# Feed-forward entries in halves, one split on GpSimd, and a narrower z panel in a two-layer hybrid block

## What is computed

```python
def first_block(x, positions, ...):
    h = x
    for l in range(DEPTH):                       # DEPTH = 2
        h = layer_norm(DEEPNORM_ALPHA * h + 0.5 * swiglu(h, ffn1_w_gate[l], ffn1_w_up[l], ffn1_w_down[l]), ...)
        mix = hybrid_mixer(h, cos, sin, w_in[l], ...)
        h = layer_norm(DEEPNORM_ALPHA * h + mix, ln2_g[l], ln2_b[l])
        h = layer_norm(DEEPNORM_ALPHA * h + 0.5 * swiglu(h, ffn2_w_gate[l], ffn2_w_up[l], ffn2_w_down[l]), ...)
    return h

def swiglu(x, w_gate, w_up, w_down):
    return (jax.nn.silu(x @ w_gate) * (x @ w_up)) @ w_down

def hybrid_mixer(x, ...):
    proj = x @ w_in                              # 1024 x 6856, cut by column
    (dq, dk, dv, dz, da, dbeta, glu, c_q, c_kv, k_r, gate_logits) = jnp.split(proj, ...)
    ...

def ada_params(c, w, b):                         # the second model's modulation
    mod = jax.nn.silu(c) @ w + b                 # c: one row of 1024; w: 1024 x 3072
```

## Time and profile before

| | |
|---|---|
| median of 3 runs | 3070.93 us (3068.96 to 3071.79) |
| the profiled execution: its own time, and its span | 3071.66 us, 3069.9 us |
| busy PE, PEld | 2913.4 us (95%), 2467.8 us (80%) |
| busy DVE, ACT, POOL | 2016.9 us (66%), 1454.4 us (47%), 50.7 us (2%) |
| mean granted TensorE clock | 0.976 |
| queue of instruction fetches | 75 packets, 1.23 MB |

### The profile page before, as it was taken

One profiled execution on the slowest core, in us unless ns is written; L12 is line 12 of the kernel. 1 busy time (PEld: TensorE's weight loads), 2 busy tenths in 40 slices (PEclk: granted clock), 3 DMA queues, 4 the chain that ended last, 5 costly groups with the idle time before them and its releaser, 6 DMA issues.

```text
span 3069.9 us, 44687 instructions
## 1 busy us (share of the span) xinstructions
PE 2913.4 (95%) x16782; PEld 2467.8 (80%) x16782; DVE 2016.9 (66%) x2457; ACT 1454.4 (47%) x1612; POOL 50.7 (2%) x93
## 2 busy tenths in 40 slices
PE   7999988899899998899999999988999999999997
PEld 7998886599899988758988699455878887888786
DVE  6767863477767788327761454144898789878987
ACT  5444521254444452214430344133776767666765
POOL 2000010000000001000000000000000000000000
PEclk9999999999899999999999999998999999999999
DMA  8754512486677433136743455313999999999995
GB/s 292 237 174 162 154 67 84 134 274 222 221 247 246 152 121 110 57 110 225 254 150 137 137 192 176 111 69 136 359 338 329 339 348 337 329 339 349 337 330 213
DMA packets 396808, 659.84 MB, mean 215 GB/s; under 512 B 12011, under 2 KB 239193, under 8 KB 396697
## 3 DMA queue, kind: packets, MB, share of 16 engines
q1 hardware_dynamic: 396696, 658.32, 62.3%
HBM read 657.23 MB, written 1.05 MB: 214 GB/s over the span
## 4 chain that ended last, share of the span: by engine, by line
PE 70%; DVE 10%; PEld 5%; issue 5%; ACT 4%; DVEq 2%; DMA 2%; PEldq 1%; ACTq 1%; SPq 0%
PE banks L711 18%; PE banks L712 17%; PE banks L713 17%; PE banks L2091 3%; PE banks L2123 3%; PE banks L1389 2%; PE banks L707 1%; PE banks L784 1%; DVE mod_sum L1045 1%; DVE expert_rest L1113 1%; PEld banks L1225 1%; DVE ffn_arena L1052 1%; PE banks L885 1%; DVE panel_rest L1740 1%; PE banks L879 1%
## 5 line engine op out<-in xcount | busy, mean ns | idle before, releaser
L711 PE MATMUL banks<-ffn_arena 128*128 128x256 f32 (+1 forms) x3460 | 1165.0, 337 | 42.8 <-DVE ffn_arena L1073 16.3
L713 PE MATMUL banks<-ffn_arena 128*128 128x256 f32 (+1 forms) x3460 | 1149.4, 332 | 0.0
L711 PEld LDWEIGHTS banks<-ffn_arena 128*128 128x128 f32 x3460 | 661.3, 191 | 117.0 <-issue 38.4
L713 PEld LDWEIGHTS banks<-ffn_arena 128*128 128x128 f32 x3460 | 660.9, 191 | 69.4
L1113 DVE TENSOR_TENSOR expert_rest<-expert_raw,ffn_arena 128x2048 fp32r<-128x2048 f32 (+1 forms) x306 | 646.4, 2161 | 85.9 <-ACT ffn_arena L972 81.5
L712 PE MATMUL banks<-ffn_arena 128*128 128x256 f32 (+1 forms) x2200 | 672.8, 306 | 0.0
L972 ACT ACTIVATE ffn_arena<-expert_raw 128x2048 fp32r<-128x2048 f32 (+1 forms) x306 | 538.9, 1815 | 110.4 <-PE banks L713 107.1
L712 PE MATMUL banks<-expert_rest,ffn_arena 128*128 128x512 f32 (+1 forms) x1224 | 465.9, 381 | 0.0
L712 PEld LDWEIGHTS banks<-ffn_arena 128*128 128x128 f32 x2200 | 423.9, 193 | 17.4 <-issue 0.5
L1052 DVE TENSOR_TENSOR ffn_arena<-gate_w,ffn_arena 128x1024 fp32r<-128x1024 f32 x110 | 130.0, 1223 | 212.0 <-ACT ffn_arena L908 212.0
L712 PEld LDWEIGHTS banks<-expert_rest,ffn_arena 128*128 128x128 f32 x1224 | 230.0, 188 | 42.8
(11 more groups left out here) (415 smaller groups left out, 3521.6 us busy)
## 6 DMA issues: line engine op xcount, KB each, us to landing
expert_raw<-in_moe_w_gate_dram SPq DMA_DIRECT2D x90, 1024.0 KB, 5.2
expert_raw<-in_moe_w_up_dram SPq DMA_DIRECT2D x90, 1024.0 KB, 5.4
expert_raw<-in_moe_w_down_dram SPq DMA_DIRECT2D x90, 1024.0 KB, 5.0
gate_w<-in_ffn_w_gate_dram SPq DMA_DIRECT2D x55, 1024.0 KB, 5.4
up_w<-in_ffn_w_up_dram SPq DMA_DIRECT2D x55, 1024.0 KB, 5.4
down_w<-in_ffn_w_down_dram SPq DMA_DIRECT2D x55, 1024.0 KB, 5.4
mod_unit<-in_mod_w_dram SPq DMA_DIRECT2D x48, 1024.0 KB, 5.1
panel<-in_w_in_dram SPq DMA_DIRECT2D x44, 1024.0 KB, 5.7
```

What stands on the lines that cost most here:

```text
L711: mm(out, w[0], x[0], start=start, stop=False)
L713: return mm(out, w[1], x[0], start=False, stop=stop)
```

## The change

Six things are done:

1. The loop over the two layers is written out (`for l in range(DEPTH)`) on every engine, so the waits compare against constants.
2. The second tile enters a feed-forward in halves of 512 columns: L1182 is two instructions, with a new count (`norm_half`) after the first; PE turns four blocks behind each, ACT copies each half, DVE subtracts each half.
3. The first gate panel of three of the four feed-forwards in the first model (not of the very first) is split earlier: ACT's pass stands between the layer norm's two square roots, and the low part is computed by GpSimd.
4. The modulation sums at the boundary of the two layers are no longer ahead of the turns: 12 of the 24 matmuls stand between the two tiles, 12 behind the second. ACT's copy of them, and a wait of DVE for them, now stand ahead of the first up panel.
5. The first step of each feed-forward is taken out of DVE's loop, with the modulation unit behind `unit_vec` and up low instead of ahead of them.
6. The eight logits move from the z panel (520 to 512 columns) to the last panel (192 to 200 columns, as a DMA of its own with runs of 32 bytes); their 16 matmuls are gone. One of two filler matmuls at the second entry is gone too.

```diff
-    + [("z", [("w_in", 0, D, C_Z, 520)]),
+    + [("z", [("w_in", 0, D, C_Z, PANEL)]),
        ("lora", [("w_in", 0, D, C_CQ, PANEL)]),
-       ("lora", [("w_in", 0, D, C_CQ + PANEL, C_GATE - C_CQ - PANEL)])]
+       ("rope_decay", [("w_in", 0, D, C_KR - PANEL // 4, KR_COLS), ("w_in", 0, D, C_Z + PANEL, 2 * HEADS)])]
...
-            with pool.Fori(0, DEPTH) as l:
+            for l in range(DEPTH):
...
+                for first in (l * FFN_LAYER + NS, l * FFN_LAYER + FFN_LAYER)[:2 if l + 1 < DEPTH else 1]:
+                    for i, half in enumerate((slice(0, KD // 2), slice(KD // 2, KD))):
+                        pool.wait_ge(gate_high, first * 2 + i + 1)
+                        last = nc.gpsimd.tensor_tensor(gate_parts[1][:, half, :], gate_w[:, half, :], gate_parts[0][:, half, :].bitcast(F32), ALU.subtract)
+                    last.then_inc(gate_low, 1)
...
-        def turn_h(pe, done, fill=0):
+        def turn_h(pe, done, fill=0, mod=None):
             for t in range(TT):
                 if t == 1 and fill:
                     spin(5, fill)
-                pe.wait_ge(norm_done, done + t + 1)
+                if t == 1 and mod is not None:
+                    mod_pe(pe, mod, banks[:, 0, 0:12], range(12))
+                if t == 0:
+                    pe.wait_ge(norm_done, done + 1)
                 for half in range(2):
+                    if t == 1 and half == 0:
+                        pe.wait_ge(norm_half, done // 2 + 1)
+                    elif t == 1:
+                        pe.wait_ge(norm_done, done + 2)
...
+            if mod is not None:
+                mod_pe(pe, mod, banks[:, 0, 12:24], range(12, 24)).then_inc(mod_col_done, 1)
...
         def turned_act(act, before):
-            for t in range(TT):
-                act.wait_ge(turned, before + 2 * t + 2)
-                act_fn(x_parts[0][:, :, t * P:(t + 1) * P], turned_tile(t), ACT.Copy).then_inc(x_high, 1)
+            act.wait_ge(turned, before + 2)
+            act_fn(x_parts[0][:, :, 0:P], turned_tile(0), ACT.Copy).then_inc(x_high, 1)
+            for half, done in ((slice(0, 4), x_half), (slice(4, 8), x_high)):
+                act.wait_ge(turned, before + 2 + half.stop // 4)
+                act_fn(x_parts[0][:, half, P:], turned_tile(1)[:, half, :], ACT.Copy).then_inc(done, 1)
...
-            with dve.Fori(0, NS - 1) as s:
+            gate_vec(dve, n, 1)
+            unit_vec(dve, n, 0, FB * SEQ)
+            up_vec(dve, n, 1)
+            if m is not None:
+                mod_vec(dve, m, 1, slice(MOD_COLS, 2 * MOD_COLS))
+            down_vec(dve, n, 0)
+            dve.wait_ge(unit_high, n + 1)
+            tt(unit_parts[1], act_t, unit_parts[0].bitcast(F32), ALU.subtract).then_inc(act_ready, 1)
+            with dve.Fori(1, NS - 1) as s:
                 step(s)
...
-            tile = v3(panel_ready(5), 0, KD, 520)
-            for t in range(TT):
-                for k in range(KD):
-                    mm(small_bank[:, 8 * t:8 * t + 8], HT[:, k, t * P:(t + 1) * P], tile[:, k, 512:520],
-                       start=k == 0, stop=k == KD - 1)
             pe.drain().then_inc(panel_used, 1)
...
-            with pe.Fori(0, DEPTH) as l:
+            for l in range(DEPTH):
                 n = l * FFN_LAYER
-                turn_h(pe, l * 6)
+                turn_h(pe, l * 6, mod=l * 2 - 1 if l else None)
...
-                spin(0, 2)
+                spin(0, 1)
                 ffn_pe(pe, n + NS, l * 2 + 1)
-                pe.wait_ge(norm_done, l * 6 + 7)
-                mod_pe(pe, l * 2 + 1, banks[:, 0, 0:24]).then_inc(mod_col_done, 1)
+            pe.wait_ge(norm_done, DEPTH * 6 + 1)
+            mod_pe(pe, 2 * DEPTH - 1, banks[:, 0, 0:24]).then_inc(mod_col_done, 1)
...
-                std_act(act, l * LN_LAYER + 2, LN_EPS)
+                std_act(act, l * LN_LAYER + 2, LN_EPS, [0])
                 gate_act(act, n + NS, 0)
+                std_act(act, l * LN_LAYER + 2, LN_EPS, [1])
                 turned_act(act, l * 12 + 8)
                 ffn_act(act, n + NS)
-                std_act(act, l * LN_LAYER + 3, 4 * LN_EPS)
-                mod_act(act, l * 2 + 1, banks[:, 0, 0:24])
+                std_act(act, l * LN_LAYER + 3, 4 * LN_EPS, [0])
+                if l + 1 < DEPTH:
+                    act.wait_ge(down_done, n + 2 * NS + 1)
+                    gate_act(act, n + FFN_LAYER, 0)
+                std_act(act, l * LN_LAYER + 3, 4 * LN_EPS, [1])
```

More of the change, by code:

```diff
@@ L575, in _ @@
                           (mod[:, 0].rearrange("o (k p) n -> p (o k) n", p=P), l * 2), first_extra)
-                for use, (_, pieces) in enumerate(MIXER_PANELS):
+                for use, (use_name, pieces) in enumerate(MIXER_PANELS):
                     if use in SPLIT_USES:
@@ L579, in _ @@
                     else:
[L580 removed]
+                        panel_load(pieces, l * MIX_USES + use, use % 2, l, use_name)
                     if use == 4:
@@ L2219, in _ @@
             act_fn(small[:, 320:324], banks[:, 3, 160:164], ACT.Copy).then_inc(col_ready, 1)
-            with act.Fori(0, DEPTH) as l:
+            for l in range(DEPTH):
                 n = l * FFN_LAYER
-                gate_act(act, n, 0)
+                if l == 0:
+                    gate_act(act, n, 0)
                 turned_act(act, l * 12)
+                if l:
+                    mod_act(act, l * 2 - 1, banks[:, 0, 0:24])
                 ffn_act(act, n)
@@ L2344, in _ @@
             dve.drain().then_inc(norm_done, TT)
+            dve.drain().then_inc(norm_half, 1)
             dve.wait_ge(setup_row, 112)
@@ L2349, in _ @@
             dve.wait_ge(col_ready, 1)
-            with dve.Fori(0, DEPTH) as l:
+            for l in range(DEPTH):
                 n = l * FFN_LAYER
-                gate_vec(dve, n, 0)
+                if l == 0:
+                    gate_vec(dve, n, 0)
                 turned_vec(dve, l * 2)
+                if l:
+                    dve.wait_ge(mod_col_done, l * 2)
                 ffn_vec(dve, n, l * 2)
```

43 lines of the change are left out of this document (27 added, 16 removed).

## The result

The kernel after takes 3029.8 us in the median of 4 runs (3025.3 to 3034.2), the kernel before, on the same chip, 3069.9 (3065.8 to 3071.8). The ratio is 0.9871, with a 95% interval from 0.985 to 0.9892: 40 us faster. The forecast was 3043.2 with a range from 3032 to 3057. The profiled execution takes 3033.03 us, its span 3031.3; before had 3071.66 and 3069.9.

What follows compares the result with a forecast made beforehand. PE carries 70% of the chain of waits, so only places where PE waits pay. Terms -7.2, -10.8, -2.4, -5.0, -2.0 and -0.7 sum to -28.1 from 3071.66; forecast 3043.2 us, range 3032 to 3057.

Steps and rivals of the forecast that it cites:

- Step 0, -7.2: First step of the four feed-forwards: PE's waits of 1.70 to 1.88 us for the up panel go whole, -7.2 us.
- z panel, -10.8: Mixer's z panel: narrow logit passes and the half-clock stretch behind them go, 5.4 us a layer, -10.8 us.
- the mixer gives nothing back: Rival: the chain behind the low-rank panel is bound by something fixed, the 10.8 us are lost, 3054 us; chance 0.18.
- GpSimd and the norm: Three entries: a GpSimd product holds DVE's norm instructions with two SBUF operands; gains 7.4 us held, 11.4 if not.
- double hold: Rival: GpSimd holds DVE over both halves; both second entries go from -1.2 to +1.0 us, 3047.6 us; chance 0.15.
- missing hold: Rival: GpSimd does not hold DVE; second entries -2.1 us each, second layer's start -7.2, 3039 us; chance 0.13.
- Slow code: Rival: written-out second layer's code is fetched late, PE stalls 2.76 us at a packet, 20 stalls give 3098; chance 0.03.
- Second entries, -2.4: Second feed-forwards' entries: without DVE's gate low part, PE starts at 599.5 instead of 600.72; -1.2 us each, -2.4.
- Second layer's start, -5.0: Second layer's start: table load and jump idle leave the path, late modulation sets gate(0) at 803.6 instead of 808.57; -5.0 us.
- Written-out loop, -2.0: Outer loop on all engines: waits against constants replace register instructions, 1.0 us a mixer, -2.0; ends 0 and -6.
- Half-clock stretches: Clock at half speed: the z panel's 3.4 us stretch goes, 1.7 us lost a layer; other stretches move by 3.4 us each.
- The remaining 0.06: Chance of 0.06 left over from forecast and rivals, spread between 3025 and 3071 us for half-clock stretches that move.

Runs made afterwards that it cites:

- b_loop_pe: Kernel before with the outer loop over the layers written out on TensorE alone; median 3066.6 us, ratio 0.9986 to before.
- a_again: The kernel after run once more with nothing changed; median 3026.6 us.
- b_loop: Kernel before with the outer loop over the layers written out on all five engines, nothing else; median 3051.1 us, ratio 0.9942 to before.
- b_loop_act: Kernel before with the outer loop written out on ScalarE alone, the other four keeping theirs; median 3061.7 us, ratio 0.9971 to before.

## Why the forecast was short

At equal clock the change is worth 30.7 us (3063.9 - 3033.2). The other 9.5 us go with the mean clock, 0.9773 before and 0.9817 after. The forecast's sum was 28.1, of which 3.4 was the z panel's half-clock time, so it had 24.7 for the first and 3.4 for the second. It was short by 6.0 in its terms and by 6.1 in the clock. Either alone would have left the time at 3037, inside the range; and the kernel after's first four runs passed the range's end by 2.2 us only, while all eight have a median of 3027.0.

- *Step 0, -7.2: right and slightly small.* The gaps went whole, nothing was late next, and each gave 2.0 to 2.1 where the second feed-forwards had the full clock, against 1.8 of idle. I take the rest for latency that goes with a gap. Four make 8.3.
- *z panel, -10.8: right.* 8.3 to 10.1 at equal clock, where the forecast without its half-clock time had 7.4, and the half-clock stretch was the passes'. The rival that the mixer gives nothing back is out.
- *GpSimd and the norm: right.* One product holds one DVE instruction: 1.28 became 3.18 and 0.75 became 2.60. The double hold and the missing hold are both out.
- *Slow code: out.* PE has the same gaps of over 0.6 us in the second layer's mixer as in the first's, none of them new, and 72 packets of instructions were fetched, before 75.
- *Second entries, -2.4: small.* The first turn to the gate went from 10.2 to 8.06 us, 2.1 each. Less a delay of the turns themselves, 1.7 and 2.0 are left, 3.7.
- *Second layer's start, -5.0: 4.2, and not for the reason given.* ScalarE's jump and table load were rightly in this term, and the modulation's second half was rightly late. But the loop alone gives 5.6 here. The forecast compared the kernel after with before, never with a kernel that only has the plain loop, and so it credited the modulation's new place and GpSimd with a gain where they give nothing or lose up to 1.4. Its reading of the clock there was short too: the trace of before is at half clock without a break from 793.6 to 814.1, also between the two windows.
- *Written-out loop, -2.0: the term that was mis-sized.* Besides the second layer's start, ScalarE's first cast starts 1.45 us sooner, since the table load at the loop's head (10.64, 1.28 us) goes there too. I had put 0.1 of cost on that entry. The four other engines' loops give 6.7 at equal clock, where I had 1.0 a mixer: about 1.5 a mixer on PE, 1.8 at the second layer's start, and the rest without a place. The loop alone gives 11.8 at equal clock, of which 5.6 lie at the second layer's start, inside the term above. Outside it are 6.2, 1.4 of them at the first gate, where this term had 2.0.
- *Half-clock stretches: the other step that failed.* "The remaining 0.06 is spread between 3025 and 3071, for half-clock stretches that move by 3.4 us each", and the range's lower end, give them room for little. The profiled trace of before has 21 such stretches, 148 us in all, that of after 16 with 117. The mean clock then rose by 0.0045, which goes with 9.5 us, where the forecast had 3.4.

**What is known of the half-clock stretches.** One place has a cause that the runs show: the z panel (6.8 us). At the second layer's start the stretch went from 20.5 to 13.7, and to 10.2 in three of four profiles with 20 blocks between the turns; but b_loop_pe, which keeps the jump, has 13.7 there too, in two pieces. Others come and go between profiles of the same code: after and a_again, one kernel, have 3.4 us and none at 209 us, 10.2 and 3.4 near 2020.

At 15 us the profiles only seem to differ (6.8 us, 3.4 or none). The record of the clock begins between 11.3 and 24.2 us, and what lies ahead of it counts as full; but in all 18 profiles the first gate's matmuls are slow until 19.8 to 24.2. The windows below have the same columns as above, first after, then before. After, PE does 15 matmuls in 3.30 us at a clock given as 1.00. That is as slow as its 18 in 3.90 us at 0.50 before; at full clock 33 fit into 3.70 us. So the sums of half-clock time miss a few us, and the mean clock of a run can be 0.001 too high.

```profile
16.70:20.00 3.30, 3.30 (x15) 3.30 (x16) 3.21 (x4) 0.00 (x0) 2.69 (x6) 1.00 1.10 349
```
```profile
18.10:22.00 3.90, 3.90 (x18) 3.90 (x19) 3.66 (x6) 0.00 (x0) 1.39 (x11) 0.50 0.84 251
22.30:26.00 3.70, 3.70 (x33) 3.70 (x33) 1.78 (x4) 0.02 (x1) 0.00 (x0) 1.00 0.77 255
```

The mean over many runs still differs by 0.0045 (±0.0008), and no single part has it. Put alone into before, the z panel gives 0.0010 of it, step 0 0.0027, the loop 0.0025 (±0.0015). Taken alone out of after, step 0 costs nothing, GpSimd's product 0.0025; the narrow passes put back cost 0.0023.

What stays open is why the mean clock rises with the whole change. That the stalls of step 0 hold it down was tested twice, with answers that don't agree.

## What to carry to other kernels

Compare a change against the kernel with its cheapest part alone: here the plain loop, one line an engine, was worth 12 of the 31 us at equal clock, and hid that costlier edits on top of it gave nothing at the place where they were meant to. Before an edit is put behind a wait, look at what it leaves idle: 12 modulation blocks stood behind a gap of 3.4 us that had room for eight more, and moving them gave 3.4 us there. And where runs scatter with the mean clock, put the clock beside each time before reading a difference of less than 10 us.

## What the runs showed of the chip

- ScalarE stands 2.6 to 2.8 us at this outer loop's jump back with nothing to wait for, and a table load of 1.28 us stands at the loop's head, on the first pass too. The five profiled kernels with a loop on ScalarE have 2.56 to 2.77 us at the jump. The SiLU line has 50 table loads before and 40 in b_loop, b_loop_act and the kernel after; the ten cost nothing that shows.
- A DVE instruction with two operands in SBUF waits for the GpSimd product that has begun and goes before the next one: 3.18 us instead of 1.28, 2.60 instead of 0.75. L1211 at the second layer's start came when little of the first product was left, and took 1.41 for 1.28; GpSimd's second product waited for it in turn (5.63 us for two of 2.36). L1203, with one operand in PSUM, is not held (1.21 us beside a product).
- 32 passes of 8 columns take 3.7 us at full clock and up to 5.3 when it falls among them. A stretch of 3.4 or 6.8 us at half clock begins 1.9 to 4.7 us after the first of them, in the middle of dense work.
- One kernel's time moves by 2.14 us for 0.001 of mean granted clock; a mean lower by 0.001 means 6.1 us more at half clock (0.002 of 3070 us), so by this estimate about a third of a stretch's length is lost.
